# A branch moved ahead of the last expert, and a fifth modulation chunk accumulated on VectorE

## The chip, the cores and the metric

The kernel runs on one core of a Trainium2 chip. Its time is the device time in microseconds (us) of one launch. Engines are named as in the profile: PE is TensorE (PEld its weight load), DVE VectorE, ACT ScalarE, POOL GpSimd, SP SyncE, which issues most of the loads.

## The reference, cut to what matters

Two transformer blocks run one after the other on 256 tokens of width 1024, all in float32. The first needs a modulation vector from the condition `c`, attention with a short convolution, and a mixture of 32 experts of which each token takes two:

```python
mod = silu(c) @ w_mod + b_mod                       # 1024 -> 6 x 1024; w_mod is 24 MB
hx  = rms_norm(x, norm1_g) * (1 + sc1) + sh1        # the first third of mod
q, k, v, b, g, u = in_proj(hx, w_in)                # attention and a 3-tap convolution
x   = x + gt1 * merge_out(attend(q, k, v), short_conv(b, g, u), w_out)
hx2 = rms_norm(x, norm2_g) * (1 + sc2) + sh2
y   = sum over the 2 chosen experts e of wts * (silu(hx2 @ w_gate[e]) * (hx2 @ w_up[e])) @ w_down[e]
x   = rms_norm(x + gt2 * y, final_g)                # 32 experts, 9 MB of weights each
```

The second block (retention, stick-breaking attention, gates, a feed-forward network) follows and is not touched, but PE can start it only when the final norm of the first is ready.

## The kernel before, in words

Each engine has its own program, written out in order, and the engines are tied together by semaphores. There is no planner: the order in each program is the order of the work.

**Modulation.** `w_mod` is taken by chunks of the contraction dimension. Four chunks `W_A` carry the columns of `sh1` and `sc1`. Eight chunks `W_B` (`W_B, 0` to `W_B, 7`, 2 MB each, 128 x 4096 elements) carry the other four vectors. `modulate_B(k)` (line 1857) is the product of the condition with chunk k on PE: 32 matmuls of 128 columns, each of which the trace shows as two records, all on L1845. The first chunks don't go through PE one by one. DVE weights and adds them: `accumulated(k)` (line 1061) multiplies chunk k by its column of the condition and adds chunk k-1, so that chunk `ACC` holds the sum of chunks 0 to `ACC`; PE then takes this one chunk with a matrix of ones. Before the change `ACC` is 3: DVE accumulates chunks 0 to 3, and PE runs `modulate_B(3)` (the sum) to `modulate_B(7)`.

**Around it on DVE.** The calls `accumulated(0)` to `accumulated(2)` stand before the third row tile of queries and keys, `accumulated(3)` after the last (line 1106). Then DVE copies the turned queries and keys out (L1110, L1111, which release `qkT_ready`), takes the row maxima of the first two score pairs (`row_max`, L1117), scales the probabilities (`divided`, L1124 and L1127), and forms the convolution from the blocks of `W_U` (L1139 to L1147).

**Around it on PE.** `conv_blocks(W_GC)` (L1918), `scores(0)` and `scores(1)` (L1927), `modulate_B(3)`, `modulate_B(4)` (L1845), `conv_blocks(W_U)` (L1918), `modulate_B(5)`, `modulate_B(6)` (L1845), the head means, `modulate_B(7)`, then attention.

**Around it on SP.** Loads are issued in the order of the list `order`. A ring of six slots holds the chunks; a load waits until the chunk before it in its slot is free. Chunks that DVE reads are freed by `modB_acc`, the others by `mod_psum`. `W_B, 4` goes where `W_B, 2` was and waits for `accumulated(3)`; `W_B, 7` goes where `W_B, 3` was and waits for `modulate_B(3)`. After them come the loads of `w_out` and then the experts' weights.

**Experts.** Slots 0 to 2 take gate, up and down of an even expert, slots 3 to 5 those of an odd one. For one expert PE gathers its tokens (L2078), turns the weighted picks (L2083), runs gate and up (L2099, 64 records each), down (L2112), and adds to the result (L2119): 16 + 4 + 128 + 48 + 16 = 212 matmul records and as many weight loads. DVE makes the next picks, scales the gathered tokens, multiplies, transposes. Expert 0 and 1 stand apart, a hardware loop runs over pairs of experts, and the last pair (experts 30 and 31) stands outside it. `last_one` splits expert 31's down into two halves, each with its own load, and puts `keep_busy` (small matmuls that compute nothing that is used, L2053) into its waits.

**Further sweeps.** One sweep takes up to 32 tokens for each expert. If an expert has more, DVE writes a number above zero into `extra_i` and releases `route_ready`. Each engine loads that number into a register and, if it is above zero, loops over all experts again. With these inputs it is zero: in the trace each expert's weights are loaded once. `route_ready` is released near 199 us, long before the test.

**After the experts** DVE and ACT form the final norm from the result's PSUM banks (L1358 on), DVE scales the rows of the second block (L1382, one for each token tile, each releases `hn_ready`), PE turns them (L1837), DVE copies them out with a gain (L1375, which releases `hnT_ready`), and PE starts the second block (L2152), whose first weights SP issues once expert 30's down product is done (L555).

PE's program at the test, before the change:

```python
for h in range(2):
    expert(PAIRS - 1, h, (PAIRS - 1) * 4 + (2 * h + 1), last_one=h == 1)
pe.wait_ge(S["route_ready"], 1)
extra = pe.value_load(extra_i[0:1, 0:1], min_val=0, max_val=SWEEPS - 1)
with pe.If(extra > 0):
    ...
keep_busy(0, 16)
```

Of the kernel before, what the change touches and what calls it, by code (L numbers as in the profile page):

```python
# [67 lines left out]
def build(nc, A, out):  # L68

    ctx = ExitStack()  # L70
    with ctx:
# [215 lines left out]
        w_out = A["w_out"].rearrange("(c p) n -> p c n", p=P)  # L287

        W_A, W_B, W_KV, W_Q, W_GB, W_GC, W_U = range(7)
        ACC = 3  # L290
        order = [(W_A, 0, 0), (W_A, 1, 1), (W_A, 2, 2), (W_A, 3, 3), (W_KV, 0, 4), (W_Q, 0, 5), (W_B, 0, 0), (W_B, 1, 1),
                 (W_GB, 0, 2), (W_B, 2, 3), (W_GC, 0, 0), (W_U, 0, 1), (W_B, 3, 5), (W_B, 4, 3), (W_B, 5, 2), (W_B, 6, 0), (W_B, 7, 5)]
        columns = {W_KV: (512, 256), W_Q: (0, 512), W_GB: (768, 512), W_GC: (1280, 512), W_U: (1792, 512)}
# [727 lines left out]
        def _(v):  # L1021
# [39 lines left out]
            def accumulated(k):  # L1061

                chunk_landed(v, W_B, k)
                if k == 0:
                    v.tensor_scalar(chunk(W_B, 0), chunk(W_B, 0), condT[:, 0, 0:1], None, ALU.mult)
                else:
                    v.drain()
                    v.scalar_tensor_tensor(chunk(W_B, k), chunk(W_B, k), condT[:, k, 0:1], chunk(W_B, k - 1), ALU.mult, ALU.add)\
                        .then_inc(S["modB_acc"], 2 if k == 1 else 1)

            v.wait_ge(S["ld_vec"], 16 * (len(VEC) + 3))
            for t in range(4):
                if t == 2:
                    for k in range(ACC):
                        accumulated(k)
                lo, n = (8, 2) if t < 2 else (0, 10)
                rows = shaped(qk[:, t, 64 * lo:640], n, HD)
                v.wait_ge(S["qksq_done"], t + 1)
                v.reduce_sum(hss[:, 0:n], shaped(qk_sq[:, 64 * lo:640], n, HD), AX).then_inc(S["qksq_sum"], 1)
                if lo == 0:  # L1080
                    v.tensor_tensor(rows[:, 0:8, :], rows[:, 0:8, :], headg[:, 0:64].unsqueeze(1).to_broadcast([P, 8, HD]), ALU.mult)
                kk = rows[:, n - 2:n, :]
                v.tensor_tensor(kk, kk, headg[:, 64:128].unsqueeze(1).to_broadcast([P, 2, HD]), ALU.mult)
                v.wait_ge(S["qk_rstd"], t + 1)
                v.drain()
                last = v.tensor_tensor(rows, rows, wide(hrs[:, 0:n], n, HD), ALU.mult)
                if lo == 0:
                    v.drain()
                    parts = qk[:, t, :].rearrange("p (n a u f) -> p n a u f", n=10, a=2, u=2)
                    for ax in range(2):  # L1090
                        x1, x2 = parts[:, :, ax, 0, :], parts[:, :, ax, 1, :]
                        o = 32 * (t - 2) + 16 * ax
                        cos = K["rope_cos"][:, o:o + 16].unsqueeze(1).to_broadcast([P, 10, 16])
                        sin = K["rope_sin"][:, o:o + 16].unsqueeze(1).to_broadcast([P, 10, 16])
                        tmp = [shaped(rope_tmp[:, 160 * i:160 * i + 160], 10, 16) for i in range(4)]
                        v.tensor_tensor(tmp[0], x1, cos, ALU.mult)
                        v.tensor_tensor(tmp[1], x2, sin, ALU.mult)
                        v.tensor_tensor(tmp[2], x1, sin, ALU.mult)
                        v.tensor_tensor(tmp[3], x2, cos, ALU.mult)
                        v.drain()  # L1100
                        v.tensor_tensor(x1, tmp[0], tmp[1], ALU.subtract)
                        last = v.tensor_tensor(x2, tmp[2], tmp[3], ALU.add)
                        v.drain()
                last.then_inc(S["qk_ready"], 1)

            accumulated(ACC)

            v.wait_ge(S["qkT_psum"], 3)
            for t in range(TT):
                v.tensor_copy(qT[:, :, P * t:P * t + P], shaped(PS[:, t, :], 4, P))  # L1110
            v.tensor_copy(kT, PS[:, 2, :]).then_inc(S["qkT_ready"], 1)  # L1111

            def row_max(p):

# [711 lines left out]
        def _(pe):  # L1826
# [30 lines left out]
            def modulate_B(k):  # L1857

                if k == ACC:
                    pe.wait_ge(S["modB_acc"], ACC + 1)  # L1860
                    by = K["ones"][:, 0:32]
                else:
                    chunk_landed(pe, W_B, k)
                    by = condT[:, k, :]
                modulate(k, chunk(W_B, k), 8, 4, by, k == ACC).then_inc(S["mod_psum"], 1)
# [78 lines left out]
            pe.wait_ge(S["qkT_ready"], 1)  # L1944
            scores(0)
            scores(1)
            modulate_B(3)
            modulate_B(4)
            conv_blocks(W_U, 2 * CV)
            modulate_B(5)  # L1950
# [99 lines left out]
            def keep_busy(bank, n):  # L2050

                for _ in range(n):
                    mm(PS[:, bank, 0:P], ident, ident, start=True, stop=True, skip_group_check=True)  # L2053
# [19 lines left out]
            def expert(n, h, p, first=False, last_one=False):  # L2073

                pe.wait_ge(S["pick_ready"], p)
                for t in range(TT):
                    for gg in range(4):
                        last = mm(PS[32 * gg:32 * gg + 32, 2 * h, 0:256], pick[:, h, t, :], xrow[:, t, 256 * gg:256 * gg + 256],  # L2078
                                  start=t == 0, stop=t == TT - 1, skip_group_check=True)
                last.then_inc(S["xe_psum"], 1)  # L2080
                pe.wait_ge(S["pick_ready"], p + 1)
                for t in range(TT):
                    last = mm(PS[:, 2 * h + 1, P * t:P * t + P], pickw[:, h, t, :], ident, start=True, stop=True, skip_group_check=True)  # L2083
                last.then_inc(S["back_psum"], 1)
                if first:
                    keep_busy(3, 3)
                pe.wait_ge(S["back_ready"], n * 2 + (h + 1))
                pe.wait_ge(S["xe_ready"], n * 2 + (h + 1))
                for j in range(2):
                    s = 3 * h + j  # L2090
                    w = up_first if first and j == 1 else slots[:, s, :]
                    if first and j == 1:
                        pe.wait_ge(S["w_first"], 16)
                    else:
                        pe.wait_ge(w_full[s], n * 16 + (16 * used[s] + (0 if s == 1 else 16)))
                    for c in range(KD):
                        for gg in range(4):
                            o = FE * c + 192 * gg
                            last = mm(PS[32 * gg:32 * gg + 32, 2 * h + 1, 192 * j:192 * j + 192], xTe[:, h, c, :],  # L2099
                                      w[:, o:o + 192], start=c == 0 and j == 0, stop=c == KD - 1, skip_group_check=True)  # L2100
                    last.then_inc(S["gu_psum"], 1)
                if last_one:
                    keep_busy(0, 4)
                pe.wait_ge(S["he_ready"], n * 2 + (h + 1))
                pe.wait_ge(w_full[3 * h + 2], n * 16 + (16 * used[3 * h + 2] + 16))
                for j in range(JE):
                    if last_one and j == JE // 2:
                        keep_busy(0, 4)
                        pe.wait_ge(S["w_half"], 16)
                    for gg in range(4):  # L2110
                        o = D * j + 256 * gg
                        last = mm(PS[32 * gg:32 * gg + 32, 2 * h, 0:256], hTe[:, h, j, :],  # L2112
                                  slots[:, 3 * h + 2, o:o + 256], start=j == 0, stop=j == JE - 1, skip_group_check=True)
                last.then_inc(S["ye_psum"], 1)
                pe.wait_ge(S["y_ready"], n * 2 + (h + 1))
                for t in range(TT):
                    for gg in range(4):
                        own = slice(32 * gg, 32 * gg + 32)
                        last = mm(PS[:, 4 + gg, 256 * t:256 * t + 256], back[own, h, P * t:P * t + P], yexp[own, h, :],  # L2119
                                  start=False, stop=True, skip_group_check=True)  # L2120
                last.then_inc(S["comb_psum"], 1)
# [3 lines left out]
            with pe.Fori(1, PAIRS - 1) as it:  # L2125
                for h in range(2):
                    expert(it, h, it * 4 + (2 * h + 1))
            for h in range(2):
                expert(PAIRS - 1, h, (PAIRS - 1) * 4 + (2 * h + 1), last_one=h == 1)
            pe.wait_ge(S["route_ready"], 1)  # L2130
            extra = pe.value_load(extra_i[0:1, 0:1], min_val=0, max_val=SWEEPS - 1)
            with pe.If(extra > 0):
                with pe.Fori(0, extra) as r:
                    with pe.Fori(0, PAIRS) as it:
                        for h in range(2):
                            expert(r * PAIRS + it + PAIRS, h, r * (2 * E + 4) + it * 4 + (2 * E + 4 + 2 * h + 1))


            keep_busy(0, 16)
            for n in range(4):  # L2140
                t, h = n // 2, n % 2
                pe.wait_ge(S["hn_ready"], 1 + t)
# [538 lines left out]
```

## Time and profile before

| | |
|---|---|
| median of three runs | 1566.0 us (1564.62 to 1566.56) |
| the profiled execution, its own time | 1565.3 us |
| its span, first to last instruction | 1563.5 us |
| mean granted PE clock | 0.929 of full speed |
| PE busy | 1298.6 us (83%) |
| DVE busy | 529.7 us (34%) |
| read from memory | 445.41 MB, 286 GB/s over the span |

Times in the rows are counted from the start of the span. "Idle" in square brackets is the time in which an engine did nothing just before the group, and the arrow names what ended it; `issue` means that the engine waited for nothing that the profile shows. A granted clock of 1.00 is 2.4 GHz and 0.50 is 1.2 GHz. Branches, register loads and waits are not shown as instructions, so they are seen only as idle time.

### The profile page before, as it was taken

What the parts mean: (1) busy time and instruction counts of PE and PEld (TensorE: products, weight loads), DVE (VectorE), ACT (ScalarE), POOL (GpSimd) and SP (SyncE); (2) the same over time, 40 slices, a digit from 0 to 9 for tenths busy, and PEclk for the clock granted to TensorE, in tenths of its full rate; (3) what the DMA queues carried; (4) which work ended last, traced back from release to release, by engine and by line L of the source; (5) the groups of instructions that cost most, each with busy time, mean ns of one, the idle gap of its engine ahead of it and who ended that gap; (6) DMA issues with size and microseconds to landing.
All of it is one profiled execution on the core that took longest, in us unless ns stands there. A gap on an engine that the chain in (4) does not pass through costs nothing.

```text
span 1563.5 us, 25170 instructions
## 1 busy us (share of the span) xinstructions
PE 1298.6 (83%) x11036; PEld 841.4 (54%) x11036; DVE 529.7 (34%) x979; ACT 194.8 (12%) x400; POOL 41.1 (3%) x84
## 2 busy tenths in 40 slices
PE   5999987666766666666666899999999999999998
PEld 4685554333433333334334766558644477688843
DVE  2555422111111111111111312533446463466653
ACT  4214100000000000000000122320011210111100
POOL 1201000000000000000000100000000000000000
PEclk8999999888788888888878999999999999999999
DMA  9959899999999999999999632343344345345551
GB/s 367 373 220 322 327 403 431 428 429 432 432 431 431 428 431 432 432 432 427 431 432 417 239 109 107 113 157 111 107 161 161 108 141 182 130 147 176 176 181 54
DMA packets 82636, 447.35 MB, mean 286 GB/s; under 512 B 3932, under 2 KB 27648, under 8 KB 67984
## 3 DMA queue, kind: packets, MB, share of 16 engines
q1 hardware_dynamic: 80304, 441.20, 70.3%
q10 hardware_dynamic: 1008, 3.74, 0.6%
q0 software_dynamic: 1264, 1.55, 0.4%
q8 instruction: 45, 0.74, 0.2%
q14 instruction: 15, 0.12, 0.0%
HBM read 445.41 MB, written 1.06 MB: 286 GB/s over the span
## 4 chain that ended last, share of the span: by engine, by line
issue 86%; PE 8%; DMA 2%; DVE 2%; POOL 1%; DVEq 1%; POOLq 0%; SPq 0%; ACT 0%
PE PS L1918 3%; PE PS L1904 2%; DMA mem<-in_w_mod 2%; PE PS L1986 2%; PE PS L1845 1%; PE PS L1837 0%; PE PS L2099 0%; DVEq L1118 0%; DVE mem L1127 0%; DVE mem L1158 0%; POOL mem L639 0%; DVE mem L1117 0%; POOL mem L586 0%; PE PS L1975 0%; PE PS L1954 0%
## 5 line engine op out<-in xcount | busy, mean ns | idle before, releaser
L2099 PE MATMUL PS<-mem 128*32 128x192 f32 x4096 | 212.5, 369 | 110.5 <-DMA mem<-in_w_up 77.6
L2099 PEld LDWEIGHTS PS<-mem 128*32 128x32 f32 x4096 | 151.7, 123 | 164.2 <-DMA mem<-in_w_up 88.2
L2112 PE MATMUL PS<-mem 128*32 128x256 f32 x1536 | 137.4, 529 | 95.0 <-DMA mem<-in_w_down 88.7
L2112 PEld LDWEIGHTS PS<-mem 128*32 128x32 f32 x1536 | 62.4, 148 | 163.5 <-DMA mem<-in_w_down 96.8
L2170 PE MATMUL PS<-mem 128*128 128x256 f32 (+1 forms) x392 | 124.2, 472 | 1.0 <-issue 1.0
L2536 PE MATMUL PS<-mem 128*128 128x256 f32 x560 | 122.6, 379 | 0.0
L2152 PE MATMUL PS<-mem 128*128 128x256 f32 (+1 forms) x512 | 115.6, 387 | 0.3 <-DVE mem L1375 0.3
L1301 DVE TENSOR_TENSOR mem<-mem,PS 128x192 f32<-128x192 f32 x32 | 11.3, 354 | 307.8 <-ACT mem L787 307.8
L2536 PEld LDWEIGHTS PS<-mem 128*128 128x128 f32 x560 | 105.6, 190 | 14.2 <-ACT mem L982 0.3
L2152 PEld LDWEIGHTS PS<-mem 128*128 128x128 f32 x512 | 96.8, 190 | 17.5 <-DVE mem L1375 0.6
L2379 PE MATMUL PS<-mem 128*128 128x512 f32 x224 | 98.4, 594 | 0.7 <-ACT mem L903 0.7
L2170 PEld LDWEIGHTS PS<-mem 128*128 128x128 f32 x392 | 73.4, 190 | 42.4 <-issue 35.9
L1305 DVE TENSOR_TENSOR mem<-PS,mem 128x256 f32<-128x256 f32 x32 | 13.6, 425 | 192.7 <-PE PS L2112 192.7
L2379 PEld LDWEIGHTS PS<-mem 128*128 128x128 f32 x224 | 41.9, 190 | 53.3 <-issue 51.8
L2585 PE MATMUL PS<-mem 128*128 128x512 f32 x154 | 66.4, 592 | 0.0
L785 ACT ACTIVATE mem<-PS 128x256 f32<-128x256 f32 x32 | 12.3, 383 | 325.0 <-PE PS L2083 325.0
L2119 PE MATMUL PS<-mem 32*128 32x256 f32 x512 | 36.7, 400 | 17.6 <-DVE mem L1305 17.6
L1837 PE MATMUL PS<-mem 128*128 128x128 f32 x248 | 36.3, 286 | 16.4 <-DVE mem L1036 12.0
L787 ACT ACTIVATE mem<-PS 128x192 f32<-128x192 f32 x32 | 10.6, 330 | 312.4 <-PE PS L2099 312.4
L2585 PEld LDWEIGHTS PS<-mem 128*128 128x128 f32 x154 | 29.2, 190 | 35.9 <-issue 35.9
L1837 PEld LDWEIGHTS PS<-mem 128*128 128x128 f32 x248 | 30.0, 147 | 32.1 <-issue 20.6
L2119 PEld LDWEIGHTS PS<-mem 32*128 32x128 f32 x512 | 23.1, 184 | 37.5 <-DVE mem L1305 36.8
(347 smaller groups left out, 1361.0 us busy)
## 6 DMA issues: line engine op xcount, KB each, us to landing
mem<-in_w_gate SPq DMA_DIRECT2D x32, 3072.0 KB, 38.8
mem<-in_w_up SPq DMA_DIRECT2D x32, 3072.0 KB, 39.2
mem<-in_w_down SPq DMA_DIRECT2D x31, 3072.0 KB, 38.8
mem<-in_w_in SPq DMA_DIRECT2D x26, 2048.0 KB, 7.8
mem<-in_w_mod SPq DMA_DIRECT2D x12, 2048.0 KB, 16.9
mem<-in_w_ffn_in SPq DMA_DIRECT2D x22, 1024.0 KB, 6.6
mem<-in_w_ffn_out SPq DMA_DIRECT2D x5, 2048.0 KB, 7.9
mem<-in_w_ret_out SPq DMA_DIRECT2D x4, 2048.0 KB, 7.9
```

Source lines behind the costliest of these rows:

```text
L1837: last = pe.transpose(PS[:, bank, rows * i:rows * i + rows], s, ident[0:rows, 0:rows])
L1904: last = mm(PS[:, bank, 0:width], hT[:, c, P * t:P * t + P], w[:, c, :], start=c == 0, stop=c == KD - 1)
L1918: last = mm(PS[:, 6 + m % 2, 0:TOK], w[:, c, P * (m % 4):P * (m % 4) + P], hT[:, c, TOK:2 * TOK], start=c == 0, stop=c == KD - 1)
L1986: last = mm(PS[:, 2 + n, :], mixT[:, first + c, P * t:P * t + P], weights[:, c, CW * o:CW * o + CW], start=start and c == 0, stop=stop and ...
L2099: last = mm(PS[32 * gg:32 * gg + 32, 2 * h + 1, 192 * j:192 * j + 192], xTe[:, h, c, :], w[:, o:o + 192], start=c == 0 and j == 0, stop=c ...
L2112: last = mm(PS[32 * gg:32 * gg + 32, 2 * h, 0:256], hTe[:, h, j, :], slots[:, 3 * h + 2, o:o + 256], start=j == 0, stop=j == JE - 1, skip_ ...
L2119: last = mm(PS[:, 4 + gg, 256 * t:256 * t + 256], back[own, h, P * t:P * t + P], yexp[own, h, :], start=False, stop=True, skip_group_check ...
L2152: last = mm(PS[:, bank, off:off + n], w[:, c, col:col + P], rhs(c), start=c == 0, stop=c == KD - 1, skip_group_check=True)
L2170: last = mm(PS[:, bank, 0:width], x[:, c, :], w[:, c, :], start=product in ("m1", "m2", "m7") and c == 0, stop=product in ("m2", "m4", "m3 ...
L2379: last = mm(PS[:, bank, :], x[:, c, :], w[:, c, :], start=start and c == 0, stop=stop and c == 3, skip_group_check=True)
L2536: last = mm(PS[:, fi_bank(bank, j), 0:256], x[:, c, :], part[:, c, :], start=start and c == 0, stop=stop and c == 3, skip_group_check=True)
L2585: return mm(PS[:, bank, :], x, w, start=j == 0, stop=j == FB // 2 - 1, skip_group_check=True)
```

## The change

Two edits that do not depend on each other.

First, `ACC` goes from 3 to 4. DVE also weights and adds the fifth chunk, `W_B, 4`, right after it has copied the keys out. PE's `modulate_B(3)` is gone, and `modulate_B(4)` takes the accumulated chunk with the matrix of ones, after a wait for `modB_acc` 5. The slot of `W_B, 3` is now freed by DVE's read (`modB_acc` 5) instead of by PE. The calls of `accumulated(0)` to `accumulated(3)` stay where they are.

Second, PE waits for `route_ready`, loads the number of further sweeps and tests it between expert 30 and expert 31 instead of after expert 31. Expert 31 is now written out twice: within the branch for further sweeps, in front of the loops, and within a second branch for none, in front of the 16 `keep_busy` matmuls. The other engines' programs are as before.

```diff
--- before.py
+++ after.py
@@ -287,7 +287,7 @@
         w_out = A["w_out"].rearrange("(c p) n -> p c n", p=P)
 
         W_A, W_B, W_KV, W_Q, W_GB, W_GC, W_U = range(7)
-        ACC = 3
+        ACC = 4
         order = [(W_A, 0, 0), (W_A, 1, 1), (W_A, 2, 2), (W_A, 3, 3), (W_KV, 0, 4), (W_Q, 0, 5), (W_B, 0, 0), (W_B, 1, 1),
                  (W_GB, 0, 2), (W_B, 2, 3), (W_GC, 0, 0), (W_U, 0, 1), (W_B, 3, 5), (W_B, 4, 3), (W_B, 5, 2), (W_B, 6, 0), (W_B, 7, 5)]
         columns = {W_KV: (512, 256), W_Q: (0, 512), W_GB: (768, 512), W_GC: (1280, 512), W_U: (1792, 512)}
@@ -1071,7 +1071,7 @@
             v.wait_ge(S["ld_vec"], 16 * (len(VEC) + 3))
             for t in range(4):
                 if t == 2:
-                    for k in range(ACC):
+                    for k in range(ACC - 1):
                         accumulated(k)
                 lo, n = (8, 2) if t < 2 else (0, 10)
                 rows = shaped(qk[:, t, 64 * lo:640], n, HD)
@@ -1103,12 +1103,13 @@
                         v.drain()
                 last.then_inc(S["qk_ready"], 1)
 
-            accumulated(ACC)
+            accumulated(ACC - 1)
 
             v.wait_ge(S["qkT_psum"], 3)
             for t in range(TT):
                 v.tensor_copy(qT[:, :, P * t:P * t + P], shaped(PS[:, t, :], 4, P))
             v.tensor_copy(kT, PS[:, 2, :]).then_inc(S["qkT_ready"], 1)
+            accumulated(ACC)
 
             def row_max(p):
 
@@ -1944,7 +1945,6 @@
             pe.wait_ge(S["qkT_ready"], 1)
             scores(0)
             scores(1)
-            modulate_B(3)
             modulate_B(4)
             conv_blocks(W_U, 2 * CV)
             modulate_B(5)
@@ -2125,18 +2125,20 @@
             with pe.Fori(1, PAIRS - 1) as it:
                 for h in range(2):
                     expert(it, h, it * 4 + (2 * h + 1))
-            for h in range(2):
-                expert(PAIRS - 1, h, (PAIRS - 1) * 4 + (2 * h + 1), last_one=h == 1)
+            expert(PAIRS - 1, 0, (PAIRS - 1) * 4 + 1)
             pe.wait_ge(S["route_ready"], 1)
             extra = pe.value_load(extra_i[0:1, 0:1], min_val=0, max_val=SWEEPS - 1)
             with pe.If(extra > 0):
+                expert(PAIRS - 1, 1, (PAIRS - 1) * 4 + 3, last_one=True)
                 with pe.Fori(0, extra) as r:
                     with pe.Fori(0, PAIRS) as it:
                         for h in range(2):
                             expert(r * PAIRS + it + PAIRS, h, r * (2 * E + 4) + it * 4 + (2 * E + 4 + 2 * h + 1))
 
 
-            keep_busy(0, 16)
+            with pe.If(extra < 1):
+                expert(PAIRS - 1, 1, (PAIRS - 1) * 4 + 3, last_one=True)
+                keep_busy(0, 16)
             for n in range(4):
                 t, h = n // 2, n % 2
                 pe.wait_ge(S["hn_ready"], 1 + t)
```

## Rows read from the trace of the kernel before

**Rows 1.** The page, 40 slices of the span, busy share in tenths

```profile
PE   5999987666766666666666899999999999999998
...
DMA  9959899999999999999999632343344345345551
```

**Rows 2.** Timeline of PE, 99 to 121: start, duration, engine, line, count [idle, releaser]

```profile
99.01 3.70 PE L1845 MATMUL PS<-mem 128*32 128x128 f32 x128
102.64 14.08 PE L1918 MATMUL PS<-mem 128*128 128x256 f32 x64
```

**Rows 3.** Timeline of DVE, 81 to 107, same columns

```profile
81.53 4.48 DVE L1068 SCALAR_TENSOR_TENSOR mem<-mem 128x4096 f32<-128x4096 f32 x1 [0.16 <-issue]
...
87.13 0.68 DVE L1111 COPY mem<-PS 128x512 f32<-128x512 f32 x1
98.27 1.22 DVE L1117 TENSOR_REDUCE mem<-PS 128x2 f32<-128x1024 f32 x1 [10.46 <-PE PS L1927]
...
106.47 0.42 DVE L1139 TENSOR_TENSOR mem<-mem,PS 128x256 f32<-128x256 f32 x1 [2.72 <-PE PS L1918]
```

**Rows 4.** Load issued at 86.04: KB, microseconds to landing

```profile
mem<-in_w_mod SPq DMA_DIRECT2D x1, 2048.0 KB, 7.3
```

**Rows 5.** Timeline of PE, experts 30 and 31 and what follows

```profile
840.05 1.17 PE L2119 MATMUL PS<-mem 32*128 32x256 f32 x16 [0.54 <-DVE mem L1305]
841.15 1.07 PE L2078 MATMUL PS<-mem 128*32 128x256 f32 x16
...
843.84 2.81 PE L2099 MATMUL PS<-mem 128*32 128x192 f32 x64 [0.98 <-ACT mem L785]
848.69 2.81 PE L2099 MATMUL PS<-mem 128*32 128x192 f32 x64 [2.04 <-DMA mem<-in_w_up]
851.43 1.16 PE L2053 MATMUL PS<-mem 128*128 128x128 f32 x8
852.93 1.50 PE L2112 MATMUL PS<-mem 128*32 128x256 f32 x24 [0.34 <-DVE mem L1303]
...
856.38 1.50 PE L2112 MATMUL PS<-mem 128*32 128x256 f32 x24 [0.86 <-DMA mem<-in_w_down]
858.43 1.15 PE L2119 MATMUL PS<-mem 32*128 32x256 f32 x16 [0.55 <-DVE mem L1305]
865.64 6.32 PE L2053 MATMUL PS<-mem 128*128 128x128 f32 x32 [6.07 <-issue]
871.79 1.91 PE L1837 MATMUL PS<-mem 128*128 128x128 f32 x16
```

**Rows 6.** Timeline of DVE after the last expert

```profile
858.70 0.60 DVE L1280 TENSOR_SCALAR mem<-mem 128x128 f32<-128x128 f32 x2
859.92 2.43 DVE L1358 TENSOR_TENSOR mem<-PS,mem 128x1024 f32<-128x1024 f32 x2 [0.63 <-PE PS L2119]
...
865.35 0.78 DVE L1382 TENSOR_SCALAR mem<-mem 128x1024 f32<-128x1024 f32 x1 [0.59 <-POOL mem L627]
866.66 0.75 DVE L1382 TENSOR_SCALAR mem<-mem 128x1024 f32<-128x1024 f32 x1 [0.53 <-POOL mem L627]
...
873.30 1.89 DVE L1375 TENSOR_TENSOR mem<-PS,mem 128x512 f32<-128x512 f32 x3 [0.18 <-PE PS L1837]
```

**Rows 7.** Windows of 1 us: busy of each engine, granted PE clock, DMA share, GB/s

```profile
864.00:865.00 1.00, 0.00 (x0) 0.00 (x0) 0.37 (x3) 0.00 (x0) 0.69 (x3) 0.52 1.04 383
...
871.00:872.00 1.00, 1.00 (x11) 1.00 (x10) 0.00 (x0) 0.00 (x0) 0.00 (x0) 1.00 0.80 330
```

**Rows 8.** The same loop of matmuls at the lower clock, timeline of PE

```profile
366.66 5.35 PE L2099 MATMUL PS<-mem 128*32 128x192 f32 x64 [3.02 <-DMA mem<-in_w_up]
```

**Rows 9.** DMA queues, 863 to 864: packets, MB, share of 16 engines

```profile
q1 hardware_dynamic: 182, 0.37, 98.4%
q8 instruction: 1, 0.02, 7.0%
```

**Rows 10.** The same queue of loads, 841 to 847

```profile
q1 hardware_dynamic: 122, 2.53, 98.4%
```

## Prediction

> **What bounds the kernel now.** I read the page by slices first: the DMA engines are full from the sixth slice to the 22nd while PE mostly works at six or seven tenths, and from the 23rd on PE is full and DMA is at a third [rows 1]. So there are three stages: a start of about 200 us, the experts, which wait for their weights until about 860 us, and the second block, which is PE's work to the end. Both edits lie where two stages meet or ahead of them, so I read the timelines there.
>
> From 99 to 121 us PE has no idle time in brackets: 3.70 us of modulation, then 14 us of convolution [rows 2], then modulation again. The reader is to see that PE sets the pace here, and that DVE stands idle for 10.46 us, from 87.8 to 98.27, waiting for the scores [rows 3]. The expert loads start only after this and are released by PE, so what PE saves here moves the whole stream of expert weights, and with it everything behind.
>
> At the end of the experts PE's chain is: down of expert 31 in two halves with 0.86 us of waiting for weights, the result at 858.43, and then 6.07 us of idle time put down to "issue" before the 16 small matmuls at 865.64, which run for 6.32 us; only then come the transposes at 871.79 and the second block at 874.05 [rows 5]. That idle time waits for no semaphore. It stands exactly where the test for further sweeps is. DVE passes the same kind of load and branch between 859.3 and 859.92, in at most 0.63 us [rows 6], so the register load is not the price. PE's branch jumps over the code of two experts, 2 x 424 = 848 instructions, counting the records of matmuls and weight loads. While it stands still, one packet of 0.02 MB passes on an instruction queue, at 863 to 864 [rows 9]. I read the 6.07 us as the fetch of the code that it jumps to. The Trainium skill says the same in "Runtime: NRT & Kernel Launch", section "Instruction fetch mechanics": a taken branch whose target is outside the window fetched so far has to wait for a DMA. By that rule the stall isn't avoided by the change, only placed elsewhere, and the trace's stall and packet agree with it.
>
> **Edit one: the fifth chunk on DVE.** Removed from PE: one `modulate_B`. Two of them take 102.64 - 99.01 = 3.63 us [rows 2], one 1.8 us, all on the path. Added to DVE: one accumulation, 4.48 us as at 81.53 [rows 3]. Its chunk is issued at 86.04 and lands 7.3 us later, at 93.35 [rows 4], so it runs from about 93.4 to 97.9, inside DVE's idle stretch. Queued behind it are the row maxima, which start at 98.27 [rows 3]: they are not late. PE reaches `modulate_B(4)` at 99.01 and finds `modB_acc` 5 about 1.1 us old. If the chunk came 2 us later, PE would wait 0.9 us, and DVE's own slack of 2.7 us before 106.47 would still cover the rest. SP: `W_B, 7` is freed at 97.9 by DVE instead of at 101 by PE, 3 us earlier, and is wanted only after 120. The loads behind it are released by PE's later products and shift with PE. Sum: -1.8 us at the start of the expert stream and, because that stream is limited by bandwidth and not by a clock on the wall, -1.8 us at its end. Bounds: 0 if the accumulated chunk is late by as much as PE saved, -1.9 by the longest reading of the row.
>
> **Edit two, the gain.** With the test gone from behind expert 31, the 16 small matmuls start at once at 859.6. Eight records take about 1.16 us [rows 5], 32 take 4.6, so they are over at 864.2, before the rows are ready. Rows of the first tile are ready at 865.35 + 0.78 = 866.1, of the second at 866.66 + 0.75 = 867.4 [rows 6]. The transposes (16 records in 1.91 us, four groups of 0.48 us) then follow the rows: the third group ends at 867.95. DVE's copy of 0.69 us, at 873.30 before [rows 6], ends at 868.7, and the second block starts at 868.75 instead of 874.05. That is -5.3 us, counted from an unchanged end of expert 31.
>
> **Edit two, the loss.** The stall now stands between 841.2 and 847.3, ahead of expert 31's gather. All of it is a delay of L2078 by 6.1 us. What hides it are the waits for weights in this expert: 2.04 us before up (848.69) and 0.86 us before the second half of down (856.38) [rows 5], 2.9 us in all. At full clock: gate moves from 843.84 to 849.95, up from 848.69 to 852.75 (+4.05), and the second half of down by 4.05 - 0.86 = 3.2 us. So expert 31 ends 3.2 us later. But the clock doesn't stay up. In the same stall before the change it went from 1.00 to 0.50 near 864.0, 4.4 us into the idle time, and came back near 870.5, after about 4.9 us of matmuls [rows 7]. At the lower level (1.2 GHz) 64 records take 5.35 us instead of 2.81 [rows 8, 5]. Before the change this fell on the small matmuls, which cost nothing that the path needs; now it falls on the gather, the turned picks and part of gate. Gather and picks at half speed: +1.0 and +0.6 us, together 1.5 us before gate can start; gate part slow: 0 to 2.5 us, I take 0.9. So the end of expert 31 moves by 3.2 + 1.5 + 0.9 = 5.6 us. Last, PE is now idle for about 2 us between the small matmuls and the transposes. Where experts wait 2 to 3 us, the following group is sometimes at half clock (366.66 after 3.02 us idle) and sometimes not (848.69 after 2.04 us) [rows 8, 5]; for the transposes and the first products that is 0 to 1.7 us, I take 0.8. Sum of edit two: -5.3 + 5.6 + 0.8 = +1.1 us.
>
> The length of the stall in its new place isn't in the trace. From below: DVE's 0.63 us. From above: at 863 the loads go in small packets (182 of them carry 0.37 MB in one microsecond, 2 KB each), but at 841 to 847 in 122 packets of 2.53 MB, about 21 KB each [rows 9, 10], ten times the size, and the fetch has to get between them; I allow 10 us. I take 6.1, the row nearest to it, a jump of the same kind. The second branch, `extra < 1`, isn't taken and costs at most as much as DVE's.
>
> **Sum.** -1.8 + 1.1 = -0.7 us. The profiled execution took 1565.3 us around a span of 1563.5, and becomes 1564.6; the median of the runs shown is 0.7 higher, 1566.0, and becomes 1565.3. A change of 0.2% (3.1 us) is about what a measurement of this kernel can tell from none.
>
> **Rivals.**
> - *The two halves cancel* (the forecast), 0.58. The stall is 5 to 8 us and the clock falls. Edit two between -0.5 and +3 us by the length of the stall and by where the clock falls, total -2.3 to +1.2: 1563.7 to 1567.2.
> - *The stall is hidden ahead of expert 31*, 0.20. The fetch is short there, or the code is already in the engine. For it: the loop's backward jumps, one for each pair, show no such gap. Against it: those land in code just run, and the forward jump here is over three experts, 1272 instructions, not two. With a stall under 2 us, the wait of 2.04 us before up takes it all: -1.8 - 5.3 + 0.8 = -6.3, 1559.7 us. A fetch of 4 us at full clock gives -1.8 - 5.3 + 1.1 + 0.8 = -5.2, and 1560.8. The Trainium skill gives TensorE room for 2048 instructions in the section just named, against 512 of the other engines, by which a target 1272 instructions ahead could be in it; but the 848 that cost 6.07 us here are fewer still, so I give this little weight.
> - *The fetch waits behind the experts' large packets*, 0.15, the one on the other side. Beyond 6.1 us each microsecond of stall adds one to the end of expert 31, since the 2.9 us of cover are spent. To be slower by 3.1 us it has to reach 6.1 + 3.8 = 9.9 us. At 10 us: -1.8 + 1.1 + 3.9 = +3.2, 1569.2 us.
> - *Edit one saves nothing*, 0.07: the chunk lands late or DVE is held up, and PE waits 1.8 us for `modB_acc` 5. Total +1.1, 1567.1 us. Against it, 1.1 us of slack on one side and 2.7 on the other.
>
> Faster by over 0.2%: the second case, 0.20. Slower: the third and a little of the first, 0.16. The rest, 0.64, is within. The range from 1561.5 to 1568.5 us leaves out the ends of the second and the third case, about 2 in 10.
>
> **What the profile of the changed kernel would show.** Two groups of 64 records on L1845 instead of 128 before the convolution's 14 us, a fifth L1068 on DVE from about 93.4 to 97.9, and `w_mod`'s last chunk issued near 98; SP's first expert loads near 124.0 instead of 125.8. Gap "issue" of about 6 us before L2078 of expert 31, near 839.4; a clock of 0.50 in the microseconds after; no wait for up, little for down; expert 31's end some 3.8 us later than before in the span (5.6 - 1.8). The small matmuls right behind it, at full clock, and a wait of about 2 us for DVE's rows before the transposes. I'd be wrong on edit one if the idle time before L1845 names DVE, and on edit two if the gap before L2078 is shorter than 4 us or longer than 8.

## The result and the profile after

The changed kernel took 1568.43 us (median of 14 runs, 1565.91 to 1569.75) against 1566.28 us (median of 14, 1564.61 to 1568.9) for the kernel before: ratio 1.0014, 95% interval 1.0008 to 1.0021. It is 2.2 us slower; 0.7 us faster was forecast. The median lies inside the range of 1561.5 to 1568.5 us, by a hair and on the side that wasn't forecast. The profiled execution took 1568.59 us around a span of 1566.8.

Edit one first. The timelines of PE, DVE and SP after the change, around 100 us, answer to [rows 2] and [rows 3] (lines of the code lie one or two further down than before):

```profile
100.13 1.95 PE L1846 MATMUL PS<-mem 128*32 128x128 f32 x64
102.01 14.08 PE L1919 MATMUL PS<-mem 128*128 128x256 f32 x64
```

```profile
93.73 4.48 DVE L1068 SCALAR_TENSOR_TENSOR mem<-mem 128x4096 f32<-128x4096 f32 x1 [5.54 <-DMA mem<-in_w_mod]
99.39 1.23 DVE L1118 TENSOR_REDUCE mem<-PS 128x2 f32<-128x1024 f32 x1 [1.17 <-PE PS L1928]
```

```profile
126.76 0.66 SPq L496 DMA_DIRECT2D mem<-in_w_gate  x1
...
199.35 0.33 SPq L496 DMA_DIRECT2D mem<-in_w_gate  x1
```

and SP before:

```profile
125.81 0.60 SPq L496 DMA_DIRECT2D mem<-in_w_gate  x1
...
199.72 0.33 SPq L496 DMA_DIRECT2D mem<-in_w_gate  x1
```

There are 64 records of modulation instead of 128, with no idle time ahead of them. The fifth accumulation fits into DVE's wait and ends 1.17 us before the scores. SP's first load that PE's experts release (199.35, 199.72 before) comes 99.22 us after the start of the modulation instead of 100.71: 1.5 us of the 1.8 have arrived. The very first expert load gained next to nothing: 26.63 us after that start (126.76) instead of 26.80 (125.81), where 1.8 us were forecast. (The two profiled executions differ by 1.1 us ahead of all that is changed, so distances are compared, not places.)

Now the end of the experts, PE after the change, against [rows 5]:

```profile
838.99 1.15 PE L2119 MATMUL PS<-mem 32*128 32x256 f32 x16 [0.54 <-DVE mem L1306]
846.68 1.94 PE L2078 MATMUL PS<-mem 128*32 128x256 f32 x16 [6.54 <-issue]
848.54 1.22 PE L2083 MATMUL PS<-mem 128*128 128x128 f32 x4
850.24 0.85 PE L2099 MATMUL PS<-mem 128*32 128x192 f32 x3 [0.47 <-ACT mem L785]
852.46 6.73 PE L2099 MATMUL PS<-mem 128*32 128x192 f32 x125 [1.38 <-issue]
859.13 1.16 PE L2053 MATMUL PS<-mem 128*128 128x128 f32 x8
860.61 1.50 PE L2112 MATMUL PS<-mem 128*32 128x256 f32 x24 [0.33 <-DVE mem L1304]
862.04 1.16 PE L2053 MATMUL PS<-mem 128*128 128x128 f32 x8
863.13 1.50 PE L2112 MATMUL PS<-mem 128*32 128x256 f32 x24
865.18 1.15 PE L2119 MATMUL PS<-mem 32*128 32x256 f32 x16 [0.55 <-DVE mem L1306]
866.26 3.84 PE L2053 MATMUL PS<-mem 128*128 128x128 f32 x32
872.95 3.29 PE L1838 MATMUL PS<-mem 128*128 128x128 f32 x16 [2.85 <-DVE mem L1383]
876.56 8.69 PE L2154 MATMUL PS<-mem 128*128 128x256 f32 x39 [0.32 <-DVE mem L1376]
```

The reader is to see two stops put down to "issue". The first, 6.54 us, is the forecast one, in its new place. The second was in no step of the forecast: after three matmul records of gate PE stands for another 1.38 us. No wait for weights is left in expert 31. Behind it the small matmuls follow at once and the transposes wait 2.85 us for DVE's rows.

Two windows of 1 us with the granted clock in the third column from the end, and the instruction queue in two windows, 843 to 844 and 849 to 850, after the change:

```profile
842.00:843.00 1.00, 0.00 (x0) 0.00 (x0) 0.00 (x0) 0.00 (x0) 0.00 (x0) 0.50 0.97 418
...
856.00:857.00 1.00, 1.00 (x32) 0.73 (x28) 0.00 (x0) 0.00 (x0) 0.00 (x0) 1.00 1.05 387
```

```profile
q8 instruction: 1, 0.02, 6.7%
...
q8 instruction: 1, 0.02, 6.6%
```

The clock is at half (1.2 GHz) from about 841.6 to 855.1, over both stops and most of gate. One packet of code passes about 3 us before each stop ends: packets at 843 and 849, PE goes on at 846.7 and 852.5. From the start of expert 30's last group to the second block are 37.57 us, 34.00 before (840.05 to 874.05): the end of the experts costs 3.6 us, where 1.1 was forecast. Up to expert 30's last group 2.2 us were saved (738.86 us from the start of the modulation for 741.04), so the second block starts 1.4 us later, counted from there. The two spans differ by 3.3 us: 1.1 lie ahead of both edits and 0.8 in the second block, and for neither does an edit give a reason (the second block to the end takes 689.0 to 691.4 us over all the kernels run here).

### The profile page after: what moved, and what is told of

Same layout as the page of the kernel before. It is cut to its first block, busy times and chain, and to the rows that moved or that the text cites. A ratio compares the mean times of both kernels' runs of the same rounds, so it can differ in the third digit from the quotient of the medians.

```text
span 1566.8 us, 25045 instructions
## 1 busy us (share of the span) xinstructions
PE 1296.5 (83%) x10972; PEld 837.1 (53%) x10972; DVE 534.2 (34%) x980; ACT 195.0 (12%) x400; POOL 41.4 (3%) x84
## 4 chain that ended last, share of the span: by engine, by line
issue 86%; PE 8%; DMA 2%; DVE 2%; POOL 1%; DVEq 1%; POOLq 0%; SPq 0%; ACT 0%
PE PS L1919 3%; PE PS L1905 2%; DMA mem<-in_w_mod 2%; PE PS L1986 2%; PE PS L1846 0%; PE PS L1838 0%; PE PS L2099 0%; DVE mem L1128 0%; DVEq L1119 0%; DVE mem L1159 0%; POOL mem L639 0%; DVE mem L1118 0%; POOL mem L586 0%; PE PS L1975 0%; PE PS L1954 0%
```

## The experiments

Each ratio is to the kernel before, run on the same chip. "The second block" is the start of L2152 or its counterpart.

| kernel | median us | ratio, 95% interval |
|---|---|---|
| changed kernel | 1568.43 | 1.0014, 1.0008 to 1.0021 |
| edit one alone | 1566.13 | 1.0000, 0.9991 to 1.0009 |
| edit two alone | 1566.78 | 1.0003, 0.9994 to 1.0012 |
| before, jump over 4 instructions | 1562.21 | 0.9976, 0.9966 to 0.9986 |
| changed kernel, 128 dead records | 1564.39 | 0.9985, 0.9976 to 0.9995 |
| before, 128 dead records | 1567.10 | 1.0007, 0.9998 to 1.0016 |
| edit one alone, 128 dead records | 1563.69 | 0.9987, 0.9978 to 0.9996 |
| before, jump over 256 records | 1566.59 | one execution |
| before, jump over 512 records | 1571.76 | one execution |
| both edits, jump over 4 instructions | 1560.91 | 0.9965, 0.9951 to 0.9978 |
| both edits, test ahead of the last pair | 1561.39 | 0.9971, 0.9960 to 0.9982 |
| the same, 26 small matmuls | 1561.38 | 0.9968, 0.9956 to 0.9979 |
| the same, 26 and 128 dead records | 1561.06 | 0.9973, 0.9961 to 0.9984 |

**Each edit alone.**

```diff
# edit one alone, against the changed kernel
-            with pe.If(extra < 1):
-                expert(PAIRS - 1, 1, (PAIRS - 1) * 4 + 3, last_one=True)
-                keep_busy(0, 16)
+            keep_busy(0, 16)          # and expert 31 again ahead of the test
# edit two alone, against the changed kernel
-        ACC = 4
+        ACC = 3                       # and modulate_B(3) again on PE
```

> Edit one alone (the fifth chunk on DVE; the test stays behind expert 31). My theory: one modulate_B of 1.8 us is gone from PE's path and nothing takes its place, so the time is 1.8 us under the kernel before (1564.5 against 1566.3, ratio 0.9988), and the 6.07 us gap before the small matmuls is still there. Rival: the edit saves nothing, because the stream of expert weights starts no earlier or the code behind it falls differently into the fetched pages; then the ratio is 1.000 and edit two alone has to account for all of the +2.2 us.

> Edit two alone (the test between expert 30 and expert 31; four chunks on DVE as before). My theory: the gap of about 6.5 us stands before expert 31's gather, expert 31 runs its gather and most of gate at the lower clock and stops once more within gate, and the second block starts 3.5 us later than in the kernel before, counted from expert 30's last group: 1569.8 us, ratio 1.0022. Rival: edit two costs only the +1.1 us of the forecast and the rest of what was measured comes from edit one; then 1567.4 us, ratio 1.0007.

Neither came out as I expected. Edit one alone gained nothing (ratio 1.0000), and edit two alone came out at +0.5 us (interval -0.9 to +1.9, so it isn't told from none), not 3.5. Each alone fits its rival's ratio. Together they measured slower than the sum, by 0.0011, which is within what the three intervals leave open. It is the timelines of PE that show what happened. Edit one alone, behind expert 31:

```profile
846.95 5.34 PE L2099 MATMUL PS<-mem 128*32 128x192 f32 x64 [3.62 <-DMA mem<-in_w_up]
...
865.66 4.88 PE L2053 MATMUL PS<-mem 128*128 128x128 f32 x24 [6.21 <-issue]
871.72 1.16 PE L2053 MATMUL PS<-mem 128*128 128x128 f32 x8 [1.17 <-issue]
```

The second stop is here too, in a kernel whose test stands where it always stood, after 24 records of small matmuls: it came with edit one. That is the second clause of this run's rival, code that falls differently into the fetched pages. (In this execution the clock was also at half for up, 5.34 us against 2.81. In the kernel before, too, up takes 2.81 us for one expert and 5.35 for another; whether edit one has a part in it here isn't shown.) Edit two alone:

```profile
846.76 1.93 PE L2078 MATMUL PS<-mem 128*32 128x256 f32 x16 [6.51 <-issue]
848.63 1.22 PE L2083 MATMUL PS<-mem 128*128 128x128 f32 x4
850.33 7.38 PE L2099 MATMUL PS<-mem 128*32 128x192 f32 x128 [0.47 <-ACT mem L785]
857.63 1.16 PE L2053 MATMUL PS<-mem 128*128 128x128 f32 x8
```

No second stop, though I expected one here: gate and up run through in 7.38 us, and the next group starts 7.30 us after their start, against 8.89 us in the changed kernel (850.24 to 859.13). The stop with what hangs on it is 1.6 us. From expert 30's last group (839.11) to the second block (875.09) this run takes 35.98 us, 2.0 more than the kernel before; 1.1 of that is given back in this pair of executions because expert 30's down, ahead of that group, ran in 4.25 us for 5.35 before, with less of it at half clock.

**What the 6 us are.** The loops left out of the branch's body, so that the jump is short:

```diff
             with pe.If(extra > 0):
-                with pe.Fori(0, extra) as r:
-                    ...
+                keep_busy(0, 1)
```

> The kernel before, with PE's loops over further sweeps left out of the branch's body (one small matmul stands in their place; PE leaves out the further sweeps, which these inputs don't need). The load of the number, the test and the jump stay where they were, behind expert 31, but the jump is over 4 instructions instead of 848. My theory: the 6.07 us are the fetch of the code that is jumped to, so the gap falls to under 0.7 us (DVE's 0.63), the small matmuls start at 860.3 at full clock, and the time falls by about 5 us to 1561.3 us, ratio 0.9968. Rival: the gap is the register load or the branch itself on PE; then it stays at 6 us and the ratio is 1.000.

```profile
859.25 1.15 PE L2119 MATMUL PS<-mem 32*128 32x256 f32 x16 [0.55 <-DVE mem L1305]
860.46 3.84 PE L2053 MATMUL PS<-mem 128*128 128x128 f32 x32
867.01 1.09 PE L1837 MATMUL PS<-mem 128*128 128x128 f32 x8 [2.71 <-DVE mem L1382]
```

Load, test and jump are all there, and the small matmuls start at 860.46, 0.06 us after the last group's end (859.25 + 1.15), with no idle time noted. The register load and the branch are not the price. The ratio is 0.9976, 3.8 us, for about 5 expected. In the profiled execution the second block starts 4.2 us earlier and then takes 1.0 us longer (690.45 us to the end for 689.45); why it does stays open. The stall was the distance.

**How far is too far.** Bodies of 64 and of 128 small matmuls that never run, one execution each:

```diff
-                keep_busy(0, 1)
+                keep_busy(0, 64)      # the other run: keep_busy(0, 128)
```

> As the short jump (PE leaves out the further sweeps, which these inputs don't need), but the branch's body is 64 small matmuls that never run, 256 records of matmuls and weight loads, one fetched packet's worth. My theory: what counts is whether the target has been fetched; the packet after the one in use has, so a jump of 256 lands in it and there is no stop before the small matmuls; the stop comes at most 6 us later, when the packet after that is wanted. Rival: any jump that leaves the packet in use stops PE for 6 us.

> The same with 128 small matmuls that never run, 512 records, two packets' worth. My theory: the target lies behind everything that has been fetched, so the gap of about 6 us is back before the small matmuls, as with the 848 records of the kernel before, and PE's clock falls to half in it. Rival: the length of the gap grows with the distance; then it is about 3.6 us here (6.07 x 512 / 848).

PE behind the test, jump over 256 records:

```profile
862.51 1.27 PE L2053 MATMUL PS<-mem 128*128 128x128 f32 x9 [0.20 <-issue]
868.53 4.71 PE L2053 MATMUL PS<-mem 128*128 128x128 f32 x23 [4.75 <-issue]
```

and over 512:

```profile
867.03 2.29 PE L2053 MATMUL PS<-mem 128*128 128x128 f32 x9 [6.06 <-issue]
873.09 5.07 PE L2053 MATMUL PS<-mem 128*128 128x128 f32 x23 [3.77 <-issue]
```

With 256 PE goes on after 0.20 us and stops 9 records later for 4.75 us; with 512 it stands 6.06 us first, as for 848, and then 3.77 us at the same record. The gap doesn't grow with distance: it is there or it isn't. Nor does it need the loops, which neither body has. I read the two rows so: the target lies in both runs at the same place in its packet of 256 instructions, 9 small matmul records and their weight loads before its end, since the two bodies differ by one packet. In the first case that packet had been fetched, in the second it had not; and in both the next one came about 6 us later (6.2 us from the jump to 868.53, 6.06 us from 867.03 to 873.09). The two single times, 1566.59 and 1571.76 us, are 5.2 us apart. In this one execution a jump over only 256 records, with its target in the wrong place, took as long as the kernel before with its 848 (1566.12 us).

The Trainium skill states the rule in "Runtime: NRT & Kernel Launch", section "Instruction fetch mechanics": code comes in blocks of 16 KiB or 256 instructions, strictly in order, and a taken branch out of the window of two has to wait. The runs agree, with 6 us for a block while the loads keep the DMA engines full; what a block takes while they are idle no run shows. The room for 2048 instructions that the section gives TensorE is of no help to a forward jump of 512.

**Where the target lies.** Dead code at the top of the branch's body moves what stands behind it by half a packet and makes the jump 128 records longer; nothing else changes:

```diff
             with pe.If(extra > 0):
+                keep_busy(0, 32)      # 128 records, never run
```

> The changed kernel with 32 small matmuls (128 records of matmuls and weight loads, what edit one took out of PE's program) added at the top of the branch for further sweeps. They never run; they only move the code behind the branch back by half of the 256 instructions that one fetched packet of 16 KB holds. My theory: the second stop, 1.38 us within the gate of expert 31 after 3 records, comes from the end of the first fetched packet, and edit one put it there by shortening the program. Then the 128 gate and up records run in one group of 7.4 us as in the run with edit two alone, expert 31 ends 1.5 us earlier, and the time is 1.5 us under the changed kernel: 1566.9 us, ratio 1.0004. Rival: the stop has to do with the weights, the register or the clock, not with where the code lies; then it stays and the ratio is 1.0014.

> The kernel before with the same 128 records that never run at the top of the branch's body. My theory: the code behind the jump now lies as in the run with edit one alone, so the small matmuls stop for about 1.2 us after 24 of their 32 records, and the second block starts 1.2 us later: ratio 1.0008. Rival: dead code changes nothing; one group of 32 records, ratio 1.0000.

> Edit one alone, with the same 128 records that never run, so that the code behind the jump lies as in the kernel before. My theory: edit one is worth what PE saves at 100 us once the second stop is gone: 1.5 to 1.8 us under the kernel before, 1564.4 us, ratio 0.999, and no stop within the small matmuls. Rival: edit one gains nothing for another reason (the expert stream or the clock takes it back); then the ratio is 1.000 with or without the padding.

The changed kernel with dead code, PE:

```profile
844.42 1.94 PE L2078 MATMUL PS<-mem 128*32 128x256 f32 x16 [6.44 <-issue]
...
847.99 7.67 PE L2099 MATMUL PS<-mem 128*32 128x192 f32 x128 [0.47 <-ACT mem L785]
```

The kernel before with dead code:

```profile
865.99 5.49 PE L2053 MATMUL PS<-mem 128*128 128x128 f32 x24 [6.04 <-issue]
872.20 1.16 PE L2053 MATMUL PS<-mem 128*128 128x128 f32 x8 [0.72 <-issue]
```

Edit one alone with dead code:

```profile
864.38 5.20 PE L2053 MATMUL PS<-mem 128*128 128x128 f32 x32 [6.12 <-issue]
```

All three as my theory had it: the stop vanishes from the changed kernel and from edit one alone, and appears in the kernel before, after 24 records, the same place as in edit one alone. The times follow: 1.0014 becomes 0.9985, 1.0000 becomes 0.9987, and 1.0000 becomes 1.0007 (this one's interval touches 1). Instructions that never run decide here whether the change is slower or faster. With the code's place held as in the kernel before, the two edits also add up: 0.9987 and 1.0003 make 0.9990, and 0.9985 was measured for both. In the changed kernel the step is larger than expected, 0.0029 or 4.5 us, where the two timelines give 1.6 us for the stop (from expert 30's last group to the second block 35.97 us against 37.57). In these two executions the padded one also reached the modulation 1.2 us sooner, ahead of both edits, took 1.0 us less from there to expert 30's last group (expert 30's down ran in 4.48 instead of 5.20 us, with less of it at half clock) and 0.75 us less in the second block. With half widths of 0.0010 and 0.0007, taken as independent, the step is 2.6 us at the least; what stands behind the microsecond or more beyond the stop stays open.

**Taking the stall away.** The short jump in the place of the change, and the real test moved where there is cover:

```diff
-            expert(PAIRS - 1, 0, (PAIRS - 1) * 4 + 1)
             pe.wait_ge(S["route_ready"], 1)
             extra = pe.value_load(extra_i[0:1, 0:1], ...)
             with pe.If(extra > 0):
-                expert(PAIRS - 1, 1, (PAIRS - 1) * 4 + 3, last_one=True)
+                last_pair()                # experts 30 and 31
                 with pe.Fori(0, extra) as r:
                     ...
             with pe.If(extra < 1):
-                expert(PAIRS - 1, 1, (PAIRS - 1) * 4 + 3, last_one=True)
+                last_pair()
                 keep_busy(0, 16)           # 26 in the second and third run
```

> Both edits, with the test between expert 30 and expert 31 as in the changed kernel, but a jump over 4 instructions (PE leaves out the further sweeps, which these inputs don't need) and expert 31 written once behind it. My theory: no stop before expert 31 and none behind it, so the second block starts when the last weights and the final norm let it: 1.8 us (edit one) and 4.0 us (what the short jump gave) under the kernel before, 1560.4 us, ratio 0.9963. Rival: the place between the experts costs something of its own (the register load waits for PE's work, gathers start late); then a gap of over 1 us stands before L2078 and the ratio is above 0.997.

> Both edits, but the test stands ahead of the last pair (before expert 30) and both of its experts are written in each branch. My theory: the gap of 6 to 7 us now falls where experts 30 and 31 still have about 3.2 + 3.1 + 2.0 + 0.9 us of waits for weights to hide it; expert 31 ends when its weights have landed, the small matmuls follow at once, and the second block starts about 5 us earlier than before from there. With 1.8 us of edit one: 6 us under the kernel before, 1560.3 us, ratio 0.996. Rival: the stall isn't hidden, since each page of code that follows the jump is fetched late too (one more stop per 256 instructions): then experts 30 and 31 both run late and the time is 1564 to 1567 us, ratio 0.999 to 1.000.

> The version with the test ahead of the last pair, with 26 small matmuls behind expert 31 instead of 16. My theory: the transposes ran at the lower clock there (3.67 us for 16 records against 1.91) because PE stood idle for 2.85 us before them; 10 more small matmuls (2.4 us) fill that, the transposes are done 1 to 1.7 us earlier, and the ratio falls from 0.9971 to 0.9962, 1560.1 us. Rival: the transposes wait for DVE's rows anyway, the clock falls or not by its own phase, and the time stays at 1561.4 us.

> The version with the test ahead of the last pair and 26 small matmuls, with 128 records that never run at the top of the branch for further sweeps, so that the second stop (1.8 us within expert 30's gate) goes. My theory: most of that stop was already hidden in expert 30's waits for weights, so the gain is small, 0 to 1 us: 1560.6 to 1561.4 us, ratio 0.9963 to 0.9968. Rival: the padding is worth as much as in the changed kernel, 2 to 4 us, and the ratio falls under 0.995.

PE with the short jump in the changed kernel's place:

```profile
837.68 1.15 PE L2119 MATMUL PS<-mem 32*128 32x256 f32 x16 [0.54 <-DVE mem L1306]
838.89 1.07 PE L2078 MATMUL PS<-mem 128*32 128x256 f32 x16
```

There is no idle time before L2078, and the ratio is 0.9965, about what edit one (0.9987) and the stall (0.9976) add up to: no other cost of the new place shows, within the interval of 0.0014 to each side. With the test ahead of the last pair, PE:

```profile
822.57 1.94 PE L2078 MATMUL PS<-mem 128*32 128x256 f32 x16 [6.36 <-issue]
...
828.00 8.20 PE L2099 MATMUL PS<-mem 128*32 128x192 f32 x125 [1.02 <-issue]
837.61 2.80 PE L2112 MATMUL PS<-mem 128*32 128x256 f32 x48 [1.41 <-DVE mem L1304]
...
855.48 1.50 PE L2112 MATMUL PS<-mem 128*32 128x256 f32 x24 [0.55 <-DMA mem<-in_w_down]
857.53 1.15 PE L2119 MATMUL PS<-mem 32*128 32x256 f32 x16 [0.55 <-DVE mem L1306]
858.60 3.84 PE L2053 MATMUL PS<-mem 128*128 128x128 f32 x32
865.30 3.67 PE L1838 MATMUL PS<-mem 128*128 128x128 f32 x16 [2.85 <-DVE mem L1383]
868.90 16.38 PE L2159 MATMUL PS<-mem 128*128 128x256 f32 x69
```

Both stops are there, the second in expert 30's gate, and expert 30 is late by some 3.4 us (its down starts at 837.61, 834.17 before). But expert 31 waits for its weights again before its second half of down, so all the lateness has been taken up, and the second block starts 5.2 us earlier than before. Ratio 0.9971, 1561.39 us: 4.6 us under the kernel before and about 7 under the changed one. This version does all of the work, and it is the one to keep.

Ten more small matmuls brought the transposes back to full clock (two groups of 1.09 us), but not an earlier time, 0.9968: the last of them waits for DVE's rows at either clock.

```profile
859.70 6.07 PE L2053 MATMUL PS<-mem 128*128 128x128 f32 x52
866.39 1.09 PE L1838 MATMUL PS<-mem 128*128 128x128 f32 x8 [0.62 <-DVE mem L1383]
867.69 1.09 PE L1838 MATMUL PS<-mem 128*128 128x128 f32 x8 [0.20 <-DVE mem L1383]
```

Dead code took the stop out of expert 30's gate (128 records in one group of 7.57 us) and did nothing further for the time (0.9973): a stop that is hidden needs no cure.

## Why the prediction was wrong

- *Edit one, -1.8 us*: right in its mechanism and size where it was made. PE lost 64 matmul records and as many weight loads, no wait took their place, the chunk landed and was added in time. With the code's place held fixed it is worth 0.0013 of the time, 2.0 us (0.6 to 3.4).
- *The step that failed*: the sum of edit two's loss has no term for a second stop behind the jump, and edit one was priced with "and, because that stream is limited by bandwidth and not by a clock on the wall, -1.8 us at its end" as its whole effect. Taking 128 records out of PE's program also moved all of its later code by half a packet. The target of the far jump came to lie some 50 records before the end of its packet, and PE reached that end before the next packet had come: 1.38 us of idle time, 1.6 us with what hangs on it. With the target moved back by dead code the same two edits measured 2.3 us faster (0.9985, 0.8 to 3.8 us), not 2.2 us slower. I counted the instructions that the jump passes, and not how many are left in the packet in which it lands.
- *Edit two, the gain, -5.3 + 0.8 us*: right, a little smaller. From expert 31's end to the second block 14.47 us became 10.23 (866.33 to 876.56), 4.2 us less for 4.5 forecast. The idle 2 us were 2.85, and the transposes ran at half clock (3.29 us), as allowed for.
- *Edit two, the loss, +5.6 us*: the mechanism right, its size too small by 2.2 us. From expert 30's last group to expert 31's end 19.53 us became 27.34, +7.8. Of the difference about 0.5 us is the first stop (6.54 for 6.1) and 1.6 us the second. The two terms for the clock missed in opposite directions and nearly cancel, which is luck: gather and picks took 0.9 us more for 1.5 forecast (from L2078 to gate 3.56 us for 2.69), gate and up 1.75 for 0.9 (7.30 us without the second stop for 5.55), because the clock came back 8.4 us after PE had gone on and not 4.9.
- *The large packets* of the experts' loads made the fetch longer by little: 6.54 against 6.07 us. That rival is out. So is the one that the stall would be hidden, or that PE's larger room would hold the target: a target 512 records ahead was not there.
- *The sum*: edit two alone measured +0.5 us (-0.9 to +1.9) for +1.1, and edit one alone 0.0 us (-1.4 to +1.4) for -1.8, since it brings the second stop along wherever the test stands. The forecast's own case ended at +1.2 us; +2.2 lies outside it, and only the allowance for the rivals kept the median within the range. My signs of being wrong (a gap before L2078 under 4 or over 8 us, a wait named DVE before L1845) did not come, because both look only at what the sum already had in it.

## What to carry to other kernels

A taken branch over much code costs about 6 us here while DMA is busy, wherever it stands: put it where the engine has that much waiting ahead of it, and more than one wait to repay it, not in the last stretch that ends a stage. After such a jump count the instructions to the end of the fetched block, since PE can run dry a second time. When two edits that should not touch give more or less together than apart, look at what each does to the place of the code behind it, and pad once with instructions that never run before believing a difference of 0.1 to 0.3%.

## What the runs showed of the hardware that I had not expected

- 128 records that never run changed the time of a 1566 us kernel from ratio 1.0014 to 0.9985, 1.6 us of it, in the timelines, by where a branch's target falls in its block of 256.
- The fetch of a block took about 6 us each time while the load queue was full: jump stalls of 6.04 to 6.97 us over 512, 848 and about 1300 to 1700 records alike (6.14 to 6.97 ahead of an expert, 6.04 to 6.21 behind the last), and packets of code 6 us apart after them (843 and 849).
- A jump over 256 records was free (0.20 us) and then cost 4.75 us 9 records later: a branch's price may stand behind its target.
